# One burst of three parts behind each inversion level's first product, rounded ones-sums, and a moved scan in a four-layer trunk

## The reference, cut to what matters

```
def step(S, inp):                       # RWKV-7, per head of 64, 16 heads
    r_t, w_t, k_t, v_t, kk_t, a_t = inp
    sa = einsum('bhvk,bhk->bhv', S, kk_t)
    S = S * w_t - sa (kk_t * a_t)^T + v_t k_t^T
    return S, einsum('bhvk,bhk->bhv', S, r_t)
...
kk = kk / maximum(norm(kk, per head), 1e-12)            # a sum over 64 channels
y_rw = head_norm(y_rw) * lnx_w + lnx_b                  # a sum over 64 channels
bonus = sum(rh * kh * r_k, per head) * vh               # a sum over 64 channels
out_rw = (y_rw + bonus) * gate
...
# odd mixer: h_t = a_t * h_(t-1) + b_t, by an associative scan over the tokens
_, hs = lax.associative_scan(_linear_combine, (a, b), axis=1)
```

## Time and profile before

| | |
|---|---|
| median of three runs | 2326.01 us |
| the profiled execution's own time | 2324.91 us |
| its span, first to last instruction | 2323.2 us |
| mean granted TensorE clock | 0.998 |
| PE busy (matmul / weight load) | 2298.0 us (99%) / 1925.6 us (83%) |
| DVE, ACT, POOL busy | 1460.5 us (63%), 1093.7 us (47%), 218.3 us (9%) |
| chain that ended last | PE 96%, DVE 2%, ACT 1%, DMA 1% |

### The profile page before, as it was taken

The page is one execution under the profiler, slowest core; times in us unless marked ns, Lnnn a source line. Parts: engine busy times, 40 slices in busy tenths (PEclk is TensorE's granted clock), DMA queues, the critical chain, the costliest instruction groups (busy, mean ns, idle before and its releaser), DMA issues.

```text
span 2323.2 us, 35488 instructions
## 1 busy us (share of the span) xinstructions
PE 2298.0 (99%) x13706; PEld 1925.6 (83%) x13706; DVE 1460.5 (63%) x1695; ACT 1093.7 (47%) x1372; POOL 218.3 (9%) x179
## 2 busy tenths in 40 slices
PE   8999999999999999999999999999999999999998
PEld 7886777778888888888888888888888888888887
DVE  5466778765675565565566577775665665665664
ACT  5455454444543444444444546755443443443443
POOL 0001033510010010010010002300100100100001
PEclk9999999999999999999999999999999999999999
DMA  7653343336666656666666655466666666666665
GB/s 232 189 164 97 111 117 111 107 120 200 183 182 202 191 177 206 189 183 200 190 190 190 183 189 180 149 197 183 180 201 196 183 197 192 190 190 192 190 191 170
DMA packets 215450, 411.54 MB, mean 177 GB/s; under 512 B 13264, under 2 KB 19792, under 8 KB 215184
## 3 DMA queue, kind: packets, MB, share of 16 engines
q1 hardware_dynamic: 213888, 407.04, 58.3%
q0 software_dynamic: 1424, 2.49, 0.4%
HBM read 407.38 MB, written 2.10 MB: 176 GB/s over the span
## 4 chain that ended last, share of the span: by engine, by line
PE 96%; DVE 2%; ACT 1%; DMA 1%; issue 0%; SPq 0%; DVEq 0%; ACTq 0%
PE acc_pair L237 19%; PE acc_pair L239 19%; PE acc_pair L238 19%; PE acc_pair L254 10%; PE tp_pair L254 10%; PE tp_pair L260 5%; PE acc_pair L260 5%; PE tp_pair L842 3%; PE acc_pair L842 2%; PE tp_pair L407 1%; DVE w_lo L226 1%; PE acc_pair L1738 1%; PE tp_pair L1738 1%; PE tp_pair L1181 1%; DMA x<-in_x_in 0%
## 5 line engine op out<-in xcount | busy, mean ns | idle before, releaser
L226 DVE TENSOR_TENSOR w_lo<-raw,w_hi 128x1024 fp32r<-128x1024 f32 (+1 forms) x760 | 1007.8, 1331 | 692.4 <-ACT w_hi L221 686.1
L221 ACT ACTIVATE w_hi<-raw 128x1024 fp32r<-128x1024 f32 (+1 forms) x760 | 800.9, 1055 | 901.8 <-PE acc_pair L239 583.6
L254 PE MATMUL acc_pair<-xT_both,w_hi 128*128 128x512 f32 x1024 | 317.9, 392 | 0.0
L254 PE MATMUL tp_pair<-xT_both,w_hi 128*128 128x512 f32 x1024 | 316.3, 390 | 0.0
L237 PE MATMUL acc_pair<-w_hi,xT_both 128*128 128x512 f32 (+1 forms) x736 | 295.7, 402 | 7.5 <-DVE w_lo L226 7.5
L238 PE MATMUL acc_pair<-w_lo,xT_both 128*128 128x512 f32 (+1 forms) x736 | 284.8, 387 | 0.0
L239 PE MATMUL acc_pair<-w_hi,xT_both 128*128 128x512 f32 (+1 forms) x736 | 284.8, 387 | 0.0
L237 PE MATMUL acc_pair<-w_hi,hidA_hi 128*128 128x512 f32 x640 | 249.8, 390 | 0.0
L239 PE MATMUL acc_pair<-w_hi,hidA_lo 128*128 128x512 f32 x640 | 249.1, 389 | 0.0
L238 PE MATMUL acc_pair<-w_lo,hidA_hi 128*128 128x512 f32 x640 | 249.0, 389 | 0.0
L237 PE MATMUL acc_pair<-w_hi,hidB_hi 128*128 128x512 f32 x624 | 244.1, 391 | 0.0
(11 more groups left out here) (275 smaller groups left out, 2313.8 us busy)
## 6 DMA issues: line engine op xcount, KB each, us to landing
raw<-in_ff_w SPq DMA_DIRECT2D x512, 512.0 KB, 4.2
raw<-in_ev_w_in SPq DMA_DIRECT2D x112, 512.0 KB, 3.7
raw<-in_od_w_in SPq DMA_DIRECT2D x64, 512.0 KB, 4.0
raw<-in_ev_w_out SPq DMA_DIRECT2D x32, 512.0 KB, 3.9
raw<-in_od_w_out SPq DMA_DIRECT2D x32, 512.0 KB, 4.1
raw<-in_ev_w_in SPq DMA_DIRECT2D x8, 288.0 KB, 5.7
x<-in_x_in SPq DMA_DIRECT2D x4, 512.0 KB, 6.6
gate_w<-in_gx_w SPq DMA_DIRECT2D x8, 256.0 KB, 2.9
```

The costliest lines, as they stand in the source:

```text
L221: act.activation(w_hi[:, j % RING, :, 0:wide], raw[:, j % RING, :, 0:wide], ACT.Copy).then_inc(hi_ready, 1)
L226: dve.tensor_tensor(w_lo[:, j % RING, :, 0:wide], raw[:, j % RING, :, 0:wide], w_hi[:, j % RING, :, 0:wide], ALU.subtract).then_inc(lo_rea ...
L254: last = nc.tensor.matmul(o[:, :], w_hi[:, j % RING, kt % KU, c * P:(c + 1) * P], both, start=(kt == 0), stop=(kt == KT - 1))
```

## The change

It has five pieces.
1. Behind the first product of levels 1 to 4 stand three parts where there were two, and none behind the update. At level 5 there are two, as before.
2. The sums over channels of `kk` and of the head norm are, but for the first block's and the last block's, computed as two float32r matmuls, of a rounded half and a remainder, as is the bonus of all blocks. ACT writes the rounded halves (`sums_hi`, `bonus_hi`), DVE the remainders (`sums_lo`, `bonus_lo`).
3. The low half of unit 2 is written ahead of `dve_variance` where it was behind it. In block 0 all low halves stand one place earlier, unit 2 in `first_front`, and eight parts are done in front of the block where there were six.
4. In group 7 of the odd layer the scan stands behind unit 3 where it was behind unit 2.
5. One unused semaphore increment goes.

```diff
         def act_front_square_hi(act, q):
+            act.activation(sums_hi[:, :], z_at(q, K_BLOCK), ACT.Square, scale=pcol_at("k_k", q)).then_inc(sem("kk_square"), 1)
         def dve_front_square_lo(dve, q):
+            dve.wait_ge(sem("kk_square"), 2 * q + 1)
+            dve.tensor_tensor(sums_lo[:, :], b_t, sums_hi[:, :], ALU.subtract).then_inc(sem("sums_low"), 1)
         def act_bonus_hi(act, p):
+            act.wait_ge(sem("bonus_in"), p + 1)
+            act.activation(bonus_hi[:, :], sq_t, ACT.Copy).then_inc(sem("bonus_hi_ready"), 1)
         def dve_bonus_lo(dve, p):
+            dve.wait_ge(sem("bonus_hi_ready"), p + 1)
+            dve.tensor_tensor(bonus_lo[:, :], sq_t, bonus_hi[:, :], ALU.subtract).then_inc(sem("bonus_lo_ready"), 1)
         def dve_square_lo(dve, n):
+            dve.wait_ge(sem("centred_square"), 2 * n + 2)
+            dve.tensor_tensor(sums_lo[:, :], csq_t, sums_hi[:, :], ALU.subtract).then_inc(sem("sums_low"), 1)
         def mm_ones(out, hi, lo):
+            mm(out, ones_r[:, :], hi[:, :], last=False)
+            return mm(out, ones_r[:, :], lo[:, :], first=False)
...
 rwkv_dve:
             if norm:
                 split_lo(dve, g, 1)
+                dve_square_lo(dve, p - 1)
...
             if norm:
+                split_lo(dve, g, 2)
                 dve_variance(dve, p - 1)
-            split_lo(dve, g, 2)
+            ahead = 0 if norm else 1
...
-                if l == 1 and norm:
-                    dve_inverse_deviation(dve, norm_own, p - 1)
+                if l == 1:
+                    if norm:
+                        dve_inverse_deviation(dve, norm_own, p - 1)
+                    else:
+                        split_lo(dve, g, 3)
                 if l == 2:
-                    split_lo(dve, g, 3)
+                    split_lo(dve, g, 3 + ahead)
...
+                    dve_bonus_lo(dve, p)
                 if l == 3:
...
+                    if front:
+                        dve_front_square_lo(dve, q)
-                    split_lo(dve, g, 4)
+                    split_lo(dve, g, 4 + ahead)
...
-            split_lo(dve, g, 5)
+            split_lo(dve, g, 5 + ahead)
...
-            split_lo(dve, g, 6)
+            if norm:
+                split_lo(dve, g, 6)
 rwkv_act:
-            split_hi(act, g, 2)
+            if norm:
+                split_hi(act, g, 2)
+            act_bonus_hi(act, p)
...
                 if l == 2:
+                    if front:
+                        act_front_square_hi(act, q)
                     split_hi(act, g, 5)
 rwkv_pe:
-                more(pe, p, parts, 2)
+                more(pe, p, parts, 3 if l < LEVELS - 1 else 2)
...
                 last.then_inc(sem("inv_done"), 1)
-                if l < LEVELS - 1:
-                    more(pe, p, parts, 1)
...
-            mm(acc[0][:, 0:T], ones, sq_t).then_inc(sem("bonus_done"), 1)
+            pe.wait_ge(sem("bonus_lo_ready"), p + 1)
+            mm_ones(acc[0][:, 0:T], bonus_hi, bonus_lo).then_inc(sem("bonus_done"), 1)
 first_front, dve and act at j == 7:
                     dve_front_key(eng, own, 0)
+                    split_lo(eng, RET_N, 2)
                     dve_front_kk(eng, own, 0)
...
                     act_front_tanh(eng, 0, acc[3], acc[3][:, T:2 * T])
+                    split_hi(eng, RET_N, 2)
                     act_front_exp(eng, 0)
 even_in and rwkv, pe:
-                more(eng, 0, parts, 6)
+                more(eng, 0, parts, 8)
...
-                parts[0] = 3
+                parts[0] = 5
 odd_side, dve:
-                    if 5 <= v <= 7 and j == 2:
+                    if 5 <= v <= 7 and j == 2 + (v == 7):
                         odd_scan(eng, v - 5)
```

More of the change, by code:

```diff
@@ L158, in trunk @@
         extra = rw("extra", [P, 4, T])
+        late = Region(low + 7 * HALVES * WIDE * 4)
+        sums_hi, sums_lo, bonus_hi = (late(n, [P, T], F32R) for n in ("sums_hi", "sums_lo", "bonus_hi"))
+        ones_r = late("ones_r", [P, P], F32R)
+        bonus_lo = Region(stg_at + 4 * T * 4)("bonus_lo", [P, T], F32R)
         rt = Region(rw_matrices)
@@ L735, in rwkv_prepare_act @@
             done = sem("lora_inputs")
+            act.activation(ones_r[:, :], con[:, CONES:CONES + P], ACT.Copy).then_inc(done, 1)
             act.activation(lora_in[0:64, 0, :], out_t[0:64], ACT.Tanh).then_inc(done, 1)
@@ L912, in pe_front_sum @@
                 pe.wait_ge(sem("gated"), q - 1)
[L913 to L914 removed]
+            if not isinstance(q, int) or q:
+                pe.wait_ge(sem("sums_low"), 2 * q - 1)
+                mm_ones(bank[:, 0:T], sums_hi, sums_lo).then_inc(sem("kk_sum_done"), 1)
+            else:
+                pe.wait_ge(sem("kk_square"), q + 1)
+                mm(bank[:, 0:T], ones, b_t).then_inc(sem("kk_sum_done"), 1)
         def pe_variance(pe, n, bank=acc[0]):
@@ L920, in pe_variance, with act_out @@
             pe.wait_ge(sem("gate_lora_landed"), 32 * (n + 1))
-            pe.wait_ge(sem("centred_square"), n + 1)
-            mm(bank[:, 0:T], ones, csq_t)
+            if n != RW_BLOCKS - 1:
+                pe.wait_ge(sem("sums_low"), 2 * n + 2)
+                mm_ones(bank[:, 0:T], sums_hi, sums_lo)
+            else:
+                pe.wait_ge(sem("centred_square"), 2 * n + 1)
+                mm(bank[:, 0:T], ones, csq_t)
             mm(bank[:, T:2 * T], lora_w[:, 1, :], lora_in[:, 2, :], last=False)
             mm(bank[:, T:2 * T], lora_w[:, 2, :], lora_in[:, 3, :], first=False).then_inc(sem("variance_done"), 1)
-        def act_out(act, n):
+        def act_out(act, n, last):
             act.wait_ge(sem("out_done"), n + 1)
@@ L931, in act_out @@
             act.activation(by_chunk(csq_t), out_turned, ACT.Square).then_inc(sem("centred_square"), 1)
+            if not last:
+                act.activation(by_chunk(sums_hi[:, :]), out_turned, ACT.Square).then_inc(sem("centred_square"), 1)
             act.activation(by_chunk(cen_t), out_turned, ACT.Copy).then_inc(sem("out_copied"), 1)
@@ L1114, in rwkv_act @@
             split_hi(act, g + 1, 0)
-            act_out(act, p)
+            act_out(act, p, not front)
             split_hi(act, g + 1, 1)
@@ L1290, in first_front @@
                     once(eng, "masks_landed", 16)
-                    once(eng, "lora_inputs", 4)
+                    once(eng, "lora_inputs", 5)
                     eng.wait_ge(stg_written, 12)
@@ L1968, in _ @@
             act.wait_ge(tables_landed, 16)
-            act.activation(junk[:, 0:1], ident[:, 0:1], ACT.Copy).then_inc(sem("act_begun"), 1)
+            act.activation(junk[:, 0:1], ident[:, 0:1], ACT.Copy)
             act.wait_ge(par_landed, 16)
```

8 lines of the change are left out of this document (added).

## The result

| | before | after |
|---|---|---|
| median of 11 runs each | 2325.44 us (2323.44 to 2326.79) | 2331.23 us (2330.45 to 2333.01) |
| profiled execution | 2324.91 us | 2331.55 us |
| its span | 2323.2 us | 2329.9 us |
| busy PE | 2298.0 us | 2288.5 us |
| busy DVE, ACT | 1460.5, 1093.7 us | 1472.2, 1102.1 us |

The ratio is 1.0027, with a 95% interval of 1.0019 to 1.0035: slower by 5.8 us. The prediction was 2333.5 us, range 2328.5 to 2337.5, and slower with a chance of 0.80.

What follows compares the result with a forecast made beforehand. PE, busy for 99% of the span, was taken as the bound. +13.1 - 1.9 - 3.9 + 0.2 = +7.5 on the profiled 2324.9 gave 2332.4, plus 1.1 for the median: 2333.5 us, range 2328.5 to 2337.5.

Steps and rivals of the forecast that it cites:

- The level waits: Inversion, 32 places: update to next first product bare at 1.02 us; each place 1.71 instead of 1.28 or 1.38; +13.1 us.
- ACT's margin of 0.11 at level 2: ACT's copy behind rounding, square and two tanh has 0.11 us left; losing it would cost 2 us or so.
- The sums: Float32r pairs save 0.19 at level 4 and 0.1 at the head norm, seven times each, bonus nothing; -1.9 us.
- The cover of DVE's remainders: Remainder ahead of the masks delays `by_key` by 0.34, covered in most blocks: costed at nothing; without margin, 2 us.
- Block 0 and around it: Earlier low halves shorten waits in and before block 0, with effects in blocks 1 and 7; -3.9 us.
- The odd layer: Group 7: PE's wait moves from unit 3 to unit 4; DVE's chain sets group 8's start; +0.2 us.
- The play of the turns: Odd layer: DVE and POOL wait in turn; scan over at 1502.9, low half of unit 4 at 1506.0.
- That changes of kind decide: Rival: 32 fewer bursts on PE save 6.4 us, sums and waits 5.6 more; 2314 us; 5% with a milder form.
- The weighty waits of the odd layer: Rival: the swap frees PE's 1.89 and the half clock, block 0 gives 5.5; +2.2, 2328 us; 10%.
- The clock: Rival: PE's stand-still of 0.6 us in each 3.9 of the inversion lowers the clock; 13 more, 2346 us; 5%.
- That the change does nothing on PE: Rival: nothing measurable on PE, needing a chain of 0.6 as if a part still covered it; 2%.

Runs made afterwards that it cites:

- Experiment 1: Kernel before, with only the moved part: three parts behind the first product of levels 1 to 4, none behind the update; 2340.08 us, ratio 1.006.
- Experiment 9: Kernel after, with ACT making the copy of the inverse twice at levels 1 to 4, PE waiting for the second; 2344.67 us, ratio 1.0085.
- experiment 8: Kernel after, with eight small low-rank input products moved from ahead of level 1 to behind its update, seven blocks; 2328.76 us, ratio 1.0014.
- experiment 10: Kernel after, with all three parts behind the update at levels 1 to 4 and none behind the first product; 2336.8 us, ratio 1.0051.
- experiment 2: Kernel after with the moved part undone: two parts behind the first product, one behind the update; the rest stays; 2318.73 us, ratio 0.9969.
- experiment 4: Kernel before with the rounded sums (piece 2) alone; 2324.93 us, ratio 0.9995.
- experiment 3: Kernel before with only the scan of group 7 in the odd layer moved behind unit 3; 2325.43 us, ratio 0.9997.
- experiment 6: Kernel of experiment 5, with ACT rounding unit 4 ahead of the decays in group 7 of the odd layer; 2316.2 us, ratio 0.9961.
- experiment 7: Kernel of experiment 6, with the scan of group 7 in the odd layer behind unit 4's low half; 2316.64 us, ratio 0.9962.
- experiment 5: Kernel of experiment 2, with DVE writing the bonus's remainder behind level 1, not level 2, in blocks 1 to 7; 2316.83 us, ratio 0.9962.

## Why the prediction was right

**The level waits (+13.1): right, a little small.** Forecast: 32 waits of about 0.6, 17 to 20 us in total, 1.02 us from update to product, 3.9 between first products. Measured: 32, 0.60, 19.0, 1.06, 3.89 (263.40 to 267.28 is 3.88). The hand-over from copy to product was 0.14, not the 0.11 read behind level 5, which makes +14.2 of the +13.1. The row of level 5 was not quite the same case: in the kernel after, its hand-over is 0.05 (copy over at 278.36, product at 278.41). Experiment 1 gave 14.2 for this piece alone. Experiment 9 shows that it is the copy that is bare, experiment 8 that the chain does not grow with work laid into it, and experiment 10 that the rule holds for the other chain too.

**ACT's margin of 0.11 at level 2: held.** Its copy started 0.53 behind the update (266.76 against 266.23), as everywhere else, and 0.48 behind the start of the second tanh, where it was 0.35 before (265.95 to 266.30). So 0.13 was to spare. The 2 us that its loss would have cost did not come.

**The sums (-1.9; its own terms give -2.0): right in sign, mis-sized.** The level-4 sum saved 0.21 (forecast 0.19). The head norm's saved 0.20, and I had taken 0.1 for a second change of kind: from its start to level 1's first product is 1.77 us, where it was 1.97. The bonus, costed at nothing, saved 0.06: from level 5's update to the next product is 0.96, where the earlier trace rows have 1.02. Together (0.21 + 0.20) x 7 + 0.06 x 8 = 3.4.

**The cover of DVE's remainders (nothing): true in this kernel, and only in this one.** In the kernel after no `inv_t` wait came, since each level is 0.44 longer. As soon as the levels are short again (experiments 2 and 4) the same 0.4 us on DVE cost up to 0.6 a block, in the blocks in which POOL works beside it. I had left POOL out there, and put this term at nothing by an argument, with no row for it.

**Block 0 and around it (-3.9): right.** Block 0 began 0.73 later; with the 0.16 by which this profile was ahead at 163.6, that is the 0.89 of the forecast for ACT's rounding ahead of the root. Of the two waits for low halves in block 0, one of 0.51 is left (forecast 0.5). Block 1 began 1.93 earlier (2.0). Block 1's wait for `by_key` became 0.9 (forecast +0.6 on 0.3), block 7's for `inv_t` went.

**The odd layer (+0.2): right, at 0.0.** The wait moved to unit 4, at 2.02, and DVE's chain set group 8. Experiments 3, 6 and 7 each tried to refute this and did not. The play of the turns came out: all had moved by 6.98 by then (transposes at 1504.27, before at 1497.29), so the scan was to end at 1509.9 and ended at 1509.97, the low half of unit 4 at 1513.0 and ended at 1512.73, 1.08 behind POOL's 1509.50 + 2.15.

**The sum.** The trace has +6.6 where I had +7.5: +1.1 by the hand-over, -1.5 by the sums, the rest by the odd layer and the ends of the program. That two terms missed by more than 1 us each and nearly cancelled is luck. The median came 2.3 below the forecast; 0.9 of that is this, and 1.4 is that I had put the median 1.1 above the profiled execution, as the first three runs had it, while after it was 0.3 below; that offset of 1.1 was chance too.

**The rivals.** That changes of kind decide is refuted by experiment 1 (a change of kind was saved at each place, some 0.2, and the bare copy cost three times as much). The weighty waits of the odd layer are refuted by experiment 7. The clock did not fall in the inversion of the kernel after: it reads 1.00 from 170 to 490 us. The reason given against this rival was weaker than it looked, since the wait of 2.04 in block 0 did end in half clock in two of the four profiles that have it (experiments 1 and 3; not before and experiment 4). That the change does nothing on PE was excluded by the 19.0 us.

## What to carry to other kernels

Filler work on TensorE is worth what it covers, not how long its bursts are: between two dependent products stands a fixed chain (here 0.53 to start, 0.38 to copy, 0.14 to hand over), and each such gap needs its own piece of filler, as long as what the chain leaves bare. A piece taken out of one gap and added to another that was already covered saved some 0.2 us in changes of kind and cost 0.67 (1.06 from start to start, less the 0.39 of the update itself). When a change bundles a loss with gains, measure it piece by piece: with the move undone, and the bonus's remainder one level earlier, the kernel takes 2316.8 us (0.4% faster than before), better than either kernel here. The odd-layer edits on top of it (2316.2 and 2316.6) add nothing that can be told from noise.

## What the runs showed of the hardware that I had not expected

- **The same idle time did not always cost the clock.** PE stood still for 2.02 us ahead of unit 4 in the kernel after, and the granted clock then read 0.74, 0.50, 0.50 in the three microseconds from 1513. In experiment 2 it stood still for 2.02 us at the same place of the program, and the clock stayed at 1.00 (first the row of the wait, then a stretch behind it):

```profile
1500.23 0.50 PE L243 MATMUL acc_pair<-w_hi,xT_both 128*128 128x512 f32 x1 [2.02 <-DVE w_lo L232]
```
```profile
1501.00:1502.00 1.00, 1.00 (x6) 0.80 (x5) 1.00 (x2) 0.88 (x1) 0.00 (x0) 1.00 0.58 88
```

  Eleven kernels have such a wait of 1.89 to 2.03 us in this group. In six the clock read 0.50 for some three microseconds behind it (before, after, experiments 3, 4, 6 and 10); in five it stayed at 1.00 (experiments 1, 2, 5, 8 and 9), and those five, and only they and experiment 7, have a wait of 1.2 us at group 8. What decides it is open. It changed no time here, since DVE sets the start of group 8.

  In block 0 it did. The kernel before and that of experiment 3 have the same program there and the same wait of 2.04; behind it the clock stayed up in the first and fell in the second, and block 0 was 37.64 us long in one and 39.14 in the other (a stretch of each, columns as above, first before, then experiment 3):

```profile
199.00:200.00 1.00, 1.00 (x25) 0.60 (x16) 0.14 (x1) 0.38 (x1) 0.00 (x0) 1.00 0.99 360
```
```profile
199.00:200.00 1.00, 1.00 (x3) 0.38 (x2) 0.00 (x0) 0.00 (x0) 0.00 (x0) 0.50 0.67 215
```

  So half clock for some three microseconds cost 1.5 us where PE sets the pace. The kernel after has no such wait in block 0. How often the clock falls there in executions of the kernel before that were not profiled, no run shows.
- **DVE and POOL lengthen each other even for small operations.** A product of two float32 tiles of 128x256 (L994) took 0.42 us in block 3 of experiment 2 and 0.96 in block 4 beside POOL's rotation. The Trainium skill ("SBUF — State Buffer", section "Who interferes with whom") describes an exclusive lock between the two, and these rows agree with it: in experiment 2 DVE's operations end 0.28 behind POOL's, and POOL's 0.59 behind DVE's (341.31 and 342.93 behind 340.72 and 342.34).
- **A second copy on the same engine, ordered by a semaphore, costs 0.42 us for 0.38 of work**: the hand-over within ACT was 0.04, from ACT to PE 0.14. Without a semaphore between them, the next operation on ACT starts 0.28 behind the copy (262.87 and 263.15 in the kernel after).
